# Merging the triangular inverses of a gated delta rule to 128 x 128 ahead of the rule, instead of solving blockwise inside it

## The reference, cut to what matters

```python
A = einsum('bhnid,bhnjd->bhnij', kb, k) * decay * strict
T = triangular_solve(eye + A, eye, lower=True, unit_diagonal=True)
u = T @ (v * beta)
w = T @ (kb * exp(gc))
...
v_new = u_n - w_n @ S
o = qd_n @ S + qk_n @ v_new
S = S * exp(gl_n) + ke_n^T @ v_new
```

## Time and profile before

| what | us |
|---|---|
| median of 3 runs | 2141.35 (2141.07 to 2141.96) |
| the profiled execution, its own time | 2141.47 |
| its span, first to last instruction | 2139.7 |
| mean granted TensorE clock, of full speed | 0.999 |
| PE busy | 2108.6 (99%) |
| DVE busy | 1492.1 (70%) |
| ACT busy | 1239.9 (58%) |
| POOL busy | 342.3 (16%) |

### The profile page before, as it was taken

One profiled execution on the slowest core, in us unless ns is written; L12 is line 12 of the kernel. 1 busy time (PEld: TensorE's weight loads), 2 busy tenths in 40 slices (PEclk: granted clock), 3 DMA queues, 4 the chain that ended last, 5 costly groups with the idle time before them and its releaser, 6 DMA issues.

```text
span 2139.7 us, 28930 instructions
## 1 busy us (share of the span) xinstructions
PE 2108.6 (99%) x9937; PEld 1744.1 (82%) x9937; DVE 1492.1 (70%) x2751; ACT 1239.9 (58%) x2391; POOL 342.3 (16%) x454
## 2 busy tenths in 40 slices
PE   7999999999999999999999999999999999999998
PEld 5888888888888888888888877887888888888886
DVE  6877777789999986668665655643666745456666
ACT  6666666677777865457555544543454555555543
POOL 3111111146566642010000000000000000000000
PEclk9999999999999999999999999999999999999999
DMA  7877667678877866666776665665665556554462
GB/s 230 236 206 212 197 193 203 185 216 246 253 204 213 232 204 219 206 236 208 268 272 240 233 203 185 195 194 162 216 224 203 187 178 197 188 166 138 158 216 99
DMA packets 430338, 439.69 MB, mean 205 GB/s; under 512 B 27472, under 2 KB 302032, under 8 KB 427792
## 3 DMA queue, kind: packets, MB, share of 16 engines
q1 hardware_dynamic: 412752, 380.97, 57.8%
q0 software_dynamic: 7600, 35.79, 4.9%
q10 hardware_dynamic: 9872, 21.50, 2.7%
HBM read 410.92 MB, written 27.28 MB: 205 GB/s over the span
## 4 chain that ended last, share of the span: by engine, by line
PE 87%; DVE 9%; issue 1%; ACT 1%; SPq 1%; POOL 1%; DMA 0%; DVEq 0%; ACTq 0%; POOLq 0%
PE pair L458 25%; PE pair L460 25%; PE pair L459 25%; DVE w_lo L439 4%; DVE QB L1063 2%; PE QA L1482 1%; SPq L397 1%; PE RA L1498 1%; PE RA L620 1%; POOL acc_p L1032 0%; PE QB L1567 0%; PE RA L796 0%; PE RA L1724 0%; PE RB L1724 0%; PE pair L480 0%
## 5 line engine op out<-in xcount | busy, mean ns | idle before, releaser
L439 DVE TENSOR_TENSOR w_lo<-raw,w_hi 128x512 fp32r<-128x512 f32 x1368 | 928.0, 698 | 408.9 <-ACT w_hi L432 408.1
L432 ACT ACTIVATE w_hi<-raw 128x512 fp32r<-128x512 f32 x1368 | 828.3, 625 | 462.9 <-PE pair L460 455.6
L458 PE MATMUL pair<-w_hi,in_hi 128*128 128x512 f32 x2336 | 935.6, 400 | 4.4 <-DVE in_lo L1126 2.8
L460 PE MATMUL pair<-w_hi,in_lo 128*128 128x512 f32 x2336 | 911.4, 390 | 0.0
L459 PE MATMUL pair<-w_lo,in_hi 128*128 128x512 f32 x2336 | 909.9, 390 | 0.0
L460 PEld LDWEIGHTS pair<-w_hi,in_lo 128*128 128x128 f32 x2336 | 438.4, 188 | 93.2
L458 PEld LDWEIGHTS pair<-w_hi,in_hi 128*128 128x128 f32 x2336 | 439.1, 188 | 92.2 <-DVE in_lo L1126 3.3
L459 PEld LDWEIGHTS pair<-w_lo,in_hi 128*128 128x128 f32 x2336 | 439.4, 188 | 86.9 <-issue 1.0
L1032 POOL TENSOR_TENSOR acc_p<-acc_p,tap 128x256 f32<-128x256 f32 x160 | 184.2, 1151 | 38.5 <-ACT tap L1006 25.1
L1006 ACT ACTIVATE tap<-upad,cwl 128x256 f32<-128x256 f32 x192 | 96.9, 508 | 51.2 <-POOL acc_p L1032 50.1
L1063 DVE SCALAR_TENSOR_TENSOR QB<-upad,cwl,QB 128x256 f32<-128x256 f32 x272 | 119.7, 479 | 0.0
(11 more groups left out here) (402 smaller groups left out, 1873.4 us busy)
## 6 DMA issues: line engine op xcount, KB each, us to landing
raw<-in_w_in_dram SPq DMA_DIRECT2D x512, 256.0 KB, 3.9
raw<-in_w_in_dram SPq DMA_DIRECT2D x80, 1024.0 KB, 5.3
raw<-in_w_out_dram SPq DMA_DIRECT2D x48, 1024.0 KB, 5.1
raw<-in_w_kv_shared_dram SPq DMA_DIRECT2D x24, 1024.0 KB, 5.0
raw<-in_w_br_a_dram SPq DMA_DIRECT2D x16, 1024.0 KB, 5.8
raw<-in_w_br_b_dram SPq DMA_DIRECT2D x16, 1024.0 KB, 6.3
raw<-in_w_mem_kv_dram SPq DMA_DIRECT2D x16, 1024.0 KB, 5.0
raw<-in_w_ple_gate_dram SPq DMA_DIRECT2D x16, 1024.0 KB, 5.0
```

Source lines behind the costliest of these rows:

```text
L432: act.activation(piece(blk, q)[0], raw[:, u, q % UK], ACT.Copy).then_inc(hi_ready[u], 1)
L439: dve.tensor_tensor(lo, raw[:, u, q % UK], hi.bitcast(F32), ALU.subtract).then_inc(lo_ready[u], 1)
L458: pe.matmul(o, xh, wh, start=(q == 0), stop=False)
L460: mm = pe.matmul(o, xl, wh, start=False, stop=(q == KC - 1))
```

## The change

After the 32 x 32 inverses are stored, two merges make 64- and then 128-wide inverses for all 32 pairs of head and tile, each before the rule begins. A merge is T_low A T_up, negated. Four heads' (or two heads') blocks are stacked along the 128 rows of one matmul; the factor in the stationary operand is block-diagonal in a buffer that POOL has zeroed, and only its diagonal blocks are loaded. The products stand in blocks B+13 and B+14, at half steps 14 and 19 of each (`MERGE_AT`): 16, then 16 + 8, with 32 columns, then 16 and 16 with 64 columns. ACT copies each result at the half step behind it. The operands come from DRAM and the results go back there, through SP, by a table of transfers that stand behind the units of the loads of j = 13, 14 and 15. In the rule a tile's solve is one group of four products, at half steps 8 and 19; the other groups move by a half step or so. The load of a group's inverse is seven DMAs in one place.

```diff
+    def factors_64_sp(sp):
+        sp.wait_ge(s["pads_ready"], 12)
+        for p, tile, a in parts_of():
+            rows = slice(SUB * p, SUB * (p + 1))
+            for c in range(2):
+                k, i = 2 * SUB * c, tile * S + 2 * SUB * c + SUB
+                sp.dma_start(m_left[rows, HALF * c:HALF * (c + 1), rows],
+                             ap_dram[a:a + HALF, k:k + SUB, i:i + SUB].rearrange("a k i -> k a i")).then_inc(s["blocks_in"], 16)
...
+    MERGE_TRANSFERS = {
+        13: {2: (solve_out_sp,), 3: (blocks_64_sp,)},
+        14: {0: (lambda sp: blocks_128_sp(sp, 0),), 1: (lambda sp: blocks_128_sp(sp, 1),), 2: (factors_128_sp,), 3: (merged_64_sp,)},
+        15: {0: (halves_128_sp,), 2: (merged_128_sp,), 3: (first_group_sp,)},
+    }
+    MERGE_AT = {(BLK_B + 13, 14): 0, (BLK_B + 13, 19): 1, (BLK_B + 14, 14): 2, (BLK_B + 14, 19): 3}
+    def merge_pe(pe, part):
+        if part == 0:
+            pe.wait_ge(s["blocks_in"], BLOCKS_64)
+            for n in range(16):
+                mm = pe.matmul(RA[:, SUB * n:SUB * (n + 1)], m_left[:, n], m_first[:, n], start=True, stop=True)
+        if part == 1:
+            pe.wait_ge(s["sv_copied"], 2 + 1)
+            for n in range(16):
+                pe.matmul(RB[:, SUB * n:SUB * (n + 1)], m_mid[:, n], m_second[:, n], start=True, stop=True)
+            for n in range(8):
+                mm = pe.matmul(RA[:, SUB * n:SUB * (n + 1)], m_diag[:, n], m_prod[:, n], start=True, stop=True)
+        if part == 2:
+            pe.wait_ge(s["halves_in"], HALVES_128)
+            pe.wait_ge(s["sv_copied"], 2 + 2)
+            for n in range(16):
+                mm = pe.matmul(bank(n, 2 * SUB), m_left[:, n], m_upper[:, n], start=True, stop=True)
+        if part == 3:
+            pe.wait_ge(s["sv_copied"], 2 + 3)
+            for n in range(16):
+                mm = pe.matmul(bank(n, 2 * SUB), m_mid[:, n], m_lower[:, n], start=True, stop=True)
+    def merge_act(act, part):
+        act.wait_ge(s["merge_on_pe"], part + 1)
...
     def rule_pe(pe, g, hs):
-        if hs == 2:
...
-                    mm = pe.matmul(four_of((RA, RB)[tile])[:, h], at_of(h, tile), t4[:, tile, h], start=True, stop=True)
-        if hs == 5:
...
-                    mm = pe.matmul(four_of((RA, RB)[tile])[:, h], x5[:, tile, h], tt4[:, tile, h], start=True, stop=True)
-        for tile, at in ((0, 7), (1, 17)):
+        for tile, at in ((0, 8), (1, 19)):
             if hs == at:
...
-            if hs == at + 2:
...
-                    mm = pe.matmul(four_of(RB)[:, h], at_of(h, tile), y2z[:, h], start=True, stop=True)
-            if hs == at + 4:
...
-                    mm = pe.matmul(four_of(RA)[:, h], tt4[:, tile, h], zneg[:, h], start=False, stop=True, skip_group_check=True)
...
-        for x in (t4, tt4):
-            pool.memset(x[:, :, :, :], 0.0).then_inc(s["pads_ready"], 1)
+        pool.memset(tt4[:, :, :, :], 0.0).then_inc(s["pads_ready"], 1)
+        for x in (m_left, m_mid, m_diag, m_upper, m_lower):
+            pool.memset(x[:, :, :], 0.0).then_inc(s["pads_ready"], 1)
...
-            if hs == 5 and blk == SOLVE_BLK + 9:
+            if hs == 14 and blk == SOLVE_BLK + 8:
                 solve_turn_act(act)
+            if (blk, hs - 1) in MERGE_AT:
+                merge_act(act, MERGE_AT[blk, hs - 1])
```

More of the change, by code:

```diff
@@ L309, in program @@
     x5 = sb("x5", [P, TT, GROUP, P])
-    zneg = sb("zneg", [P, GROUP, P])
+    spot[0] = at_s
+    m_diag = sb("m_diag", [P, 8, P])
+    m_64 = sb("m_64", [P, 16, SUB])
+    m_upper = sb("m_upper", [P, 16, 2 * SUB])
+    m_lower = sb("m_lower", [P, 16, 2 * SUB])
     oss = sb("oss", [P, TT * GROUP])
@@ new lines, in program, with halves, blocks_128_sp @@
+    BLOCKS_64 = 16 * (8 + 16 + 4)
+    def halves(to, half):
+        return lambda b: to[2 * SUB * half + SUB * b:2 * SUB * half + SUB * (b + 1)]
+    def blocks_128_sp(sp, half):
+        for tile in range(TT):
+            heads = slice(HALF * tile, HALF * (tile + 1))
+            for b in range(2):
+                cols_b = slice(SUB * b, SUB * (b + 1))
+                sp.dma_start(halves(m_upper, half)(b)[:, heads, cols_b], inverses_of(1, b, tile, HALF * half)).then_inc(s["halves_in"], 16)
+                sp.dma_start(halves(m_lower, half)(b)[:, heads, cols_b], inverses_of(0, 2 + b, tile, HALF * half)).then_inc(s["halves_in"], 16)
@@ new lines, in halves_128_sp @@
+    def halves_128_sp(sp):
+        sp.wait_ge(s["t_stored"], 32 + 16 * 12)
+        for half in range(2):
+            for tile in range(TT):
+                heads, a = slice(HALF * tile, HALF * (tile + 1)), slice(HALF * half, HALF * (half + 1))
+                sp.dma_start(halves(m_upper, half)(1)[:, heads, 0:SUB], t64_rows[tile, a].rearrange("a (i j) -> i a j", i=SUB))\
+                  .then_inc(s["halves_in"], 16)
+                sp.dma_start(halves(m_lower, half)(0)[:, heads, SUB:2 * SUB], t64_dram[1, tile, a].rearrange("a (j i) -> j a i", j=SUB))\
+                  .then_inc(s["halves_in"], 16)
@@ new lines, in program, with merged_128_sp, first_group_sp @@
+    HALVES_128 = 16 * (16 + 4 + 8)
+    def merged_128_sp(sp):
+        sp.wait_ge(s["sv_copied"], 2 + 4)
+        for half in range(2):
+            rows = slice(2 * SUB * half, 2 * SUB * (half + 1))
+            for tile in range(TT):
+                sp.dma_start(t128_dram[tile, HALF * half:HALF * (half + 1)].rearrange("a (j i) -> j a i", j=2 * SUB),
+                             m_128[rows, HALF * tile:HALF * (tile + 1)]).then_inc(s["t_stored"], 16)
+    def first_group_sp(sp):
+        sp.wait_ge(s["t_stored"], 32 + 16 * 16)
+        t_in_sp(sp, 0)
+        sp.wait_ge(s["merge_on_pe"], 4)
+        ap_in_sp(sp, 0)
@@ L795, in rule_pe @@
                 for h in range(GROUP):
[L796 to L809 removed]
+                    mm = pe.matmul(four_of(RA)[:, h], tt4[:, tile, h], vbk4[:, h, 0] if tile == 0 else r1[:, h], start=True, stop=True)
                 mm.then_inc(s["rule_on_pe"], 1)
@@ L894, in rule_dve @@
     def rule_dve(dve, g, hs):
[L895 to L905, removed]
+        for tile, at in ((0, 9), (1, 20)):
             if hs == at:
@@ L2295, in _ @@
         groups(2, 1)
-        with pe.Fori(4, KC, 2) as j:
+        with pe.Fori(4, 12, 2) as j:
             for i in range(2):
                 groups(j, i)
+        merge = lambda blk, _, hs: merge_pe(pe, MERGE_AT[blk, hs]) if (blk, hs) in MERGE_AT else None
+        for j in range(12, KC):
+            pe_block(pe, BLK_B + j, j % 2, in_hi, in_lo, beside([(group, j - 1, 1 - j % 2), (merge, BLK_B + j, 0)]))
         tail_pe(pe)
```

176 lines of the change are left out of this document (106 added, 70 removed).

## The result

| kernel | median us | range | runs |
|---|---|---|---|
| before | 2141.62 | 2141.07 to 2142.17 | 11 |
| after | 2147.55 | 2145.44 to 2148.82 | 11 |

The ratio is 1.0027, with a 95% interval of 1.0018 to 1.0035: slower by 5.9 us. The profiled execution of after took 2148.82, its span is 2147.0. The prediction said 2129.6 and faster with a chance of 0.9. It is wrong in sign and by 18 us.

The account below looks back on a forecast made before the run. PE was taken to bound the kernel, rule blocks included. From 2141.47 us: -28.5 rule products, -3.4 rule waits, +16.5 merge products, +3.5 merge waits = -11.9, so 2129.6 us, range 2124 to 2137.5.

Parts of the forecast that it names:

- The wait for the first merge: B+13, SP's queue: last small load lands at 722.0, 0.3 us before PE; wait taken as 0.5 us, between 0 and 2.
- The steps costed at nothing: POOL's longer clearing, ACT's stops and turn, eight small loads at j = 5, fewer DVE additions: no cost on the path.
- a lead of 8.2 us: At POOL's clearing: ACT and DVE are six chunks ahead of PE, covering taps that begin about 2 us late.
- ACT's turn of 2.15 us: ACT turns the last solve result behind its tap of 699.41, in a fuller stretch; the lead covers it.
- the eight small loads at j = 5: They cost SP 4 us where a weight unit has more than 10 to spare, so nothing.
- The merge products: B+13 and B+14: 72 float32 products, 144 instructions, add 16.5 us; few columns save nothing.
- The waits for the merges: PE waits for SP's loads: 0.5 us at the first merge, 3.0 at the third part (second merge), none at the others.
- Rule products and waits removed: Four rule blocks: 256 instructions fewer, -28.5 us, and DVE waits gone, -3.4 us (at least 1, at most 3.9).
- B: Rival, slower: small DMAs on SP's queue cost still more; at 0.9 us each 2151.8 us; chance 0.03.
- A: Rival: small DMAs on SP's queue cost 0.66 us each, waits grow by 2.6 and 5.2; 2137.4 us, chance 0.12.
- C: Rival: merge products cost by columns, 5.8 us instead of 16.5, waits remain; 2118.9 us, chance 0.05.
- D: Rival: rule blocks keep their waits, DVE's scaling or tt4's reload late; +3.9 us, 2133.5 us, chance 0.14.

Follow-up runs that it names:

- the last pair of runs: Against the version with both transfers early: clearing split, second merge at half steps 21 and 26; first-merge products 64 columns wide, 2127.03 us, or 32, 2130.52 us.
- the version with both transfers early: Against after: bg load and gate_a_tanh store put ahead of the merge's transfers at j = 13, 14 and 15; 2132.41 us, ratio 0.9955.
- the wide versions: Against the version with both transfers early: first-merge products 64 (2135.17 us) or 128 columns (2135.4); also 64 with split clearing and later second merge (2127.03).
- the late merge: Against the version with both transfers early: clearing split, second merge at half steps 21 and 26 of B+14, products still 32 columns; 2130.52 us, ratio 0.9951.
- clearing in pieces: Against the version with both transfers early: POOL clears tt4 and m_left at the old place, m_mid behind group 3, the rest behind group 4; 2131.17 us.

## Why the prediction was wrong, point by point

*The step that failed* is the walk along SP's queue in "The wait for the first merge". I laid the twenty small loads into SP's queue, found when the last would land, and compared this with PE's merge products alone. The walk was right in its own numbers: the loads were issued until 720.4 where I had 719.2. But behind them stand the store of `gate_a_tanh` and the load of `bg`, and the prediction never asked who waits for these. It said that PE would wait "for nothing else in these blocks". The price: 9.3 and 5.9 us of PE standing idle; and 15.1 us, half clock included, come back when the two transfers are moved. This alone turns a gain into the loss: without it 2132.41, inside the range. The cause is shown from both sides, by undoing it in after and by making it in the kernel before.

*The steps costed at nothing.* Clearing cost 1.2 us: it was said to hide behind a lead of 8.2 us, but ACT's and DVE's taps wait for the tap weights that POOL copies behind the clearing, ACT and DVE take their instructions in order, and so their work for the next block's `z2b`, on which PE waits at half step 9, comes late too. This path hasn't that lead. ACT's turn of 2.15 us and the eight small loads at j = 5 left no wait on PE.

*The merge products* were sized right, 0.218 each where I had 0.222 to 0.25. What I hadn't in the sum is what goes with 32 columns on the clock: 3.5 us by the last pair of runs. Nothing in the trace of before could show it, since it has no run of narrow products.

*The waits for the merges*, 0.5 and 3.0, didn't come in after, because PE was late by the stalls. They were there behind them: 2.5 and 3.4 us at the second merge once PE was on time. They end at 756.9 and 758.6, where the walk had 755.3 to 758.2.

*Rule products and waits removed*: 30.3 of 31.9 us. The rule blocks are 29.2 and 29.0 us long, inside the 29 to 30 forecast. Nearly all of the 1.6 that are missing is the half clock behind the stall of B+15 (0.72 in the window from 792): from that block's transposes to the end of the span after takes 1347.08 us, and the version with both transfers early, which has no such stall, 1345.54. That is 31.8 less than the 1377.37 of the kernel before.

*The sum by what was measured*, against the span: clearing 1.3, stalls 9.3 and 5.9, the rest of the first merge's distance 4.5 (13.7 less 9.2 of products, the half clock of the windows), the 1.6 of half clock behind B+15, less the 3.5 of merge waits that were forecast and didn't come: 19.1 us. The span was 19.2 us above the forecast (+7.3 instead of -11.9).

*The rivals.* B had the right side by the wrong mechanism: the sixty small DMAs cost SP 0.60 us each in the mean, not 0.9. That lies between my 0.53 and A's 0.66; the first twenty took 0.60 too, two of them 1.22 and 1.58. But A's place was not the one that decided: once the stalls were gone, the first merge waited for nothing, and the second for the 2.5 to 3.4 us of the forecast. C is out by 3.49 us for sixteen products at any width. D is out: PE has no wait in the rule blocks of after, and they take 28.6, 29.2 and 29.0 us. (The low end of my range doesn't follow from its own terms either: without waits they give 2125.6, not 2124.)

Open: what part of the chain of stalls hides behind another (moving both for j = 13 alone gave 7.0 us, for 14 and 15 the other 8.1), what about 32 columns lowers the clock, and why a short wait sometimes does. Only widths of 32, 64 and 128 in this place were run.

## What to carry to other kernels

When transfers are added to a queue, walk the queue past them to the next transfers that somebody else waits for, and price their delay by their readers, not by the new work's. Anything small and urgent (a bias, a store that frees a buffer) belongs ahead of a batch. And when a stall is taken away, ask again who is late next: here the second merge's loads stood 2.5 us behind, and only moving the merge by seven half steps made the wider products pay.

## What the runs showed of the hardware

The granted clock fell with PE never idle. In the version with both transfers early, forty products of float32 with 32 columns took it to means of 0.83 and 0.66 over two windows of 10 us; the same forty with 64 or 128 columns left it at 1.00. How far it fell differs from version to version: from the transposes of B+13 to those of B+14 the wide versions take 31.3 us, the narrow ones without a stall there 34.5 (the late merge), 34.6 (clearing in pieces) and 36.1 (both early). In PE's timeline of after, the last eight of them, from 744.35 to 747.05, took 2.70 us, and 1.79 with 128 columns (734.19 to 735.98). The Trainium skill's page "TensorE: Matmul & The Clock Gate", section "What's actually happening", says that the chip sets the clock by how busy PE has been. By the profile's busy time (10.00 of 10.00 us) the clock should have stayed up; the measurement decides, and busy time as the profile counts it doesn't tell this.

A short wait can cost more than itself, but need not. The wait of 2.48 us at 756.93 was followed by a clock of 0.83 over the next 20 us, 3.4 us more. In the version with both early for j = 13 alone, a wait of 2.38 us at nearly the same time left it at 1.00:

```profile
745.00:760.00 15.00, 12.62 (x61) 10.21 (x59) 8.18 (x17) 8.35 (x16) 3.47 (x5) 1.00 0.81 190
760.00:780.00 20.00, 20.00 (x121) 17.69 (x121) 12.21 (x25) 13.56 (x28) 10.39 (x10) 1.00 0.55 148
```

A product of float32 has one price, 0.218 us, for 32, 64 and 128 columns, when each loads its own 128 x 128 operand.
